# Dividing a conditioning product's 128 rows on VectorE over two feed-forward layers instead of three

## What is computed

```python
def _modulated_norm(h, gain, shift, scale):
    return _rms_norm(h, gain) * (1.0 + scale) + shift

def _swiglu(h, w1, w2):
    a, b = jnp.split(h @ w1, 2, axis=-1)
    return (jax.nn.silu(a) * b) @ w2

ctx = ctx + FFN_RESIDUAL * mc[2, 2] * _swiglu(
    _modulated_norm(ctx, norm_g[i, 2], mc[2, 0], mc[2, 1]), ffn_w1[i, 1], ffn_w2[i, 1])
```

## Time and profile before

| | us |
|---|---|
| median of three executions (2767.69 to 2777.02) | 2773.91 |
| the profiled execution | 2775.72 |
| its span in the trace | 2773.9 |
| up part of `mlp00` | about 66 to 298 |
| up part of `mlp01` | about 913 to 1144 |
| up part of `mlp10` | about 1281 to 1511 |

### The profile page before, as it was taken

How to read it: one execution, slowest core, us unless ns; L and a number is a source line. 1 busy time by engine, 2 the same in 40 slices (tenths; PEclk the granted TensorE clock), 3 DMA queues, 4 the chain that set the end, 5 groups by cost and what they waited for, 6 DMA issues and landing times.

```text
span 2773.9 us, 52909 instructions
## 1 busy us (share of the span) xinstructions
PE 2709.3 (98%) x21984; PEld 2390.5 (86%) x21984; DVE 1454.0 (52%) x2776; ACT 1187.2 (43%) x2123; POOL 1476.2 (53%) x809
## 2 busy tenths in 40 slices
PE   8999999999999999999999999999999999999999
PEld 6888888778888888889888896899998799898999
DVE  4777406656663676505766124453175676613560
ACT  5222225435554322224222245644445666555553
POOL 4444443444334444444444442388886377595887
PEclk9999999999999999999999999999999999999999
DMA  8665432210001455424555326265564253353465
GB/s 308 211 210 196 139 99 84 94 61 4 4 27 61 169 193 169 152 92 146 187 176 173 110 93 137 69 197 185 168 190 151 70 164 118 115 177 128 155 195 160
DMA packets 106549, 384.11 MB, mean 138 GB/s; under 512 B 11431, under 2 KB 16712, under 8 KB 104776
## 3 DMA queue, kind: packets, MB, share of 16 engines
q1 hardware_dynamic: 87880, 313.61, 35.2%
q10 hardware_dynamic: 18432, 67.12, 6.9%
HBM read 375.44 MB, written 5.24 MB: 137 GB/s over the span
## 4 chain that ended last, share of the span: by engine, by line
PE 90%; ACT 3%; DVE 2%; POOL 2%; DMA 1%; issue 1%; SPq 0%; ACTq 0%
PE bank L236 25%; PE bank L238 24%; PE bank L237 24%; PE bank L1088 2%; POOL weights_lo L229 1%; PE upper_banks L236 1%; PE upper_banks L238 1%; PE upper_banks L237 1%; PE upper_banks L1890 1%; PE upper_banks L1873 1%; PE bank L1864 1%; PE upper_banks L1065 1%; PE bank L1202 1%; PE upper_banks L1135 1%; PE upper_banks L1213 1%
## 5 line engine op out<-in xcount | busy, mean ns | idle before, releaser
L229 POOL TENSOR_TENSOR weights_lo<-weights_landing,weights_hi 128x1024 fp32r<-128x1024 f32 x554 | 1341.9, 2427 | 1147.5 <-ACT weights_hi L219 1141.0
L219 ACT ACTIVATE weights_hi<-weights_landing 128x1024 fp32r<-128x1024 f32 x554 | 587.2, 1060 | 1140.7 <-PE bank L238 1032.0
L236 PE MATMUL bank<-normed_hi,weights_lo 128*128 128x256 f32 (+1 forms) x2776 | 922.2, 332 | 6.1 <-ACT normed_hi L707 1.9
L238 PE MATMUL bank<-normed_hi,weights_hi 128*128 128x256 f32 (+1 forms) x2776 | 914.9, 330 | 0.0
L237 PE MATMUL bank<-normed_lo,weights_hi 128*128 128x256 f32 (+1 forms) x2776 | 911.7, 328 | 0.0
L236 PEld LDWEIGHTS bank<-normed_hi,weights_lo 128*128 128x128 f32 x2776 | 522.3, 188 | 66.1 <-issue 4.4
L237 PEld LDWEIGHTS bank<-normed_lo,weights_hi 128*128 128x128 f32 x2776 | 522.4, 188 | 51.6
L238 PEld LDWEIGHTS bank<-normed_hi,weights_hi 128*128 128x128 f32 x2776 | 522.3, 188 | 51.4
L236 PE MATMUL bank<-hidden_hi,weights_lo 128*128 128x256 f32 (+1 forms) x1026 | 339.1, 331 | 0.0
L238 PE MATMUL bank<-hidden_hi,weights_hi 128*128 128x256 f32 (+1 forms) x1026 | 338.6, 330 | 0.0
L237 PE MATMUL bank<-hidden_lo,weights_hi 128*128 128x256 f32 (+1 forms) x1026 | 337.3, 329 | 0.0
(11 more groups left out here) (469 smaller groups left out, 3691.9 us busy)
## 6 DMA issues: line engine op xcount, KB each, us to landing
weights_landing<-w_up SPq DMA_DIRECT2D x176, 512.0 KB, 3.5
ada_rows<-w_ada_rows ACTq DMA_DIRECT2D x128, 512.0 KB, 4.3
weights_landing<-w_down SPq DMA_DIRECT2D x88, 512.0 KB, 3.5
weights_landing<-w_dn SPq DMA_DIRECT2D x33, 512.0 KB, 3.5
weights_landing<-w_mlp_up SPq DMA_DIRECT2D x32, 512.0 KB, 3.5
weights_landing<-w_mlp_down SPq DMA_DIRECT2D x32, 512.0 KB, 3.5
weights_landing<-w_gate SPq DMA_DIRECT2D x24, 512.0 KB, 4.2
weights_landing<-w_xbc SPq DMA_DIRECT2D x24, 512.0 KB, 3.5
```

The lines of the kernel that those rows point to most:

```text
L219: k.nc.scalar.activation(k.WH[:, u % SLOTS, :], k.W[:, u % LANDS, :], ACT.Copy).then_inc(*k.AC.mark(("unit hi", u)))
L229: k.nc.gpsimd.tensor_tensor(k.WL[:, u % SLOTS, :], k.W[:, u % LANDS, :], k.WH[:, u % SLOTS, :].bitcast(F32), ALU.subtract).then_inc(*k.PO. ...
L236: nc.tensor.matmul(out, ll, rh, start=start, stop=False, skip_group_check=True)
L238: return nc.tensor.matmul(out, lh, rh, start=False, stop=stop, skip_group_check=True)
```

## The change

Two thirds of the table change, and one name in a wait of SyncE:

```diff
 ROWS_FIRST = 2 * KT
-ROWS = {"mlp00": (16, 64), "mlp01": (64, 104), "mlp10": (104, 144)}
+ROWS = {"mlp00": (16, 80), "mlp01": (80, 144)}
...
     def rope():
-        sp.wait_ge(*k.DV.after("ada mod", ROWS["mlp10"][1] // KT - 1))
+        sp.wait_ge(*k.DV.after("ada mod", ROWS["mlp01"][1] // KT - 1))
```

## The result

The changed kernel took **2794.92 us** (median; 2792.03 to 2806.58) beside 2773.91 (2767.69 to 2777.71) for the kernel before: ratio **1.0085, 95% interval 1.0057 to 1.0113**, slower by 21.0 us. The forecast was 2785, so slower by 11.0. The sign, the places and the range held; the size was half of what came. The profiled execution of after took 2792.03 us, its span is 2790.2.

What follows compares the result with a forecast made beforehand. TensorE's stream was taken to set the time, with rows free while VectorE keeps pace. Stalls and clock loss, less transposes, 2.8 + 1.7 + 6.0 + 2.2 - 1.7 = +11.0 us, gave 2784.9 on the median of 2773.91; range 2773 to 2802.

Steps and rivals of the forecast that it cites:

- The pair of 11.91 us: `mlp00` and `mlp01`, up part: a three-row pair behind another takes 11.91 us, 0.92 more than TensorE's, its transfer late.
- Lo at 0.69, a wait of 0.8 to 0.9: Sign of being right: lo at 0.69 us once lag exceeds 2, `ada_rows` waits of 0.8 to 0.9 in nearly every three-row pair.
- The lag, forecast 14.9 and 18.1: Raw's start against its undelayed start, at pair 21: 14.9 us late in `mlp00`, 18.1 in `mlp01`.
- rival A: Nothing is late, as lo shortens when GpSimd is idle and lag heals itself: -1.7 us, 2772; chance 0.10.
- the collision that the forecast had: Row transfers starting together with a load of weights, around a lag of 2.9, land later: 1.4 us taken, in `mlp00`.
- The cover of 12.1 us at lo 21: First down tile, step 21: raw 21 may start 12.1 us late before TensorE must wait for lo 21.
- The stalls: TensorE stands still waiting for lo 21: 2.8 us in `mlp00`, 6.0 in `mlp01`, some 0.7 of these at the last up tile.
- Covers that hold: Down part: the seventh unit of weights still arrives before TensorE needs it at step 48, about 4 us to spare.
- The clock, 1.7 and 2.2: TensorE at 1.2 instead of 2.4 GHz behind each stall: 1.7 us lost in `mlp00`, 2.2 in `mlp01`.
- Transposes, -1.7: `mlp10` loses its 16 transposes where TensorE is the bound: -1.7 us.
- B: Rival: the three-row pair takes 11.7 to 11.8 us, so stalls are smaller: +2.6 to +5.4, 2776 to 2780; chance 0.22.
- C: Rival: transfers land later; 0.35 us more each pair gives +24, 2798 (chance 0.14); 1.67 in all 17, +68, 2842 (0.04).

Runs made afterwards that it cites:

- the one with late short operations: The changed kernel with the short scale or gate operation moved behind lo of the next pair, ahead of that pair's rows: 2787.59 us, ratio 1.0053.
- the one with matmuls in the wait: The changed kernel with ten useless matmuls ahead of the wait for lo 21 in the first down tile of `mlp00` and `mlp01`: 2791.4 us, 1.0077.
- The kernel with 61 and 61 rows: The changed kernel with rows divided 61, 61 and 6 over `mlp00`, `mlp01` and `mlp10`: 2774.89 us, ratio 1.0011.

## Why the prediction was right in sign and half in size

**The pair of 11.91 us.** Right, a little small. The pairs of three rows behind three in after take mostly 11.9 to 12.1, 12.0 in the middle. The transfer is what is late, as said: with it a pair earlier the pair takes 10.98. The two pairs of two rows came out at 9.29 and 9.30 (forecast 9.28).

**Lo at 0.69, a wait of 0.8 to 0.9.** The lo is right, the wait was written wrongly: 2.1 to 2.4, since a lo that ends 1.3 us sooner leaves that much more to wait. The start of the first row, 4.24 after raw, is what I should have named; it is 4.2 to 4.4.

**The lag, forecast 14.9 and 18.1, measured 21.7 and 21.9.** Here the sum fails. Up to pair 2 it holds: +0.8 and +5.6 (forecast 0.8 and 5.4). From pair 2 to 21 after takes 229.68 us in `mlp00` against 208.74: +20.9, forecast 12.7 + 1.4. The 6.8 more are: the three short operations that GpSimd holds up, 1.65 + 1.08 + 1.16 = 3.9, a term that I put at nothing though rival A's own row showed the mechanism; transfers that came later than the others, by 0.6, 0.6 and 1.8 (waits of 2.78, 2.80 and 3.97 where 2.2 is usual), 3.0 for the 1.4 I had; and the rest, 1.3, is the 12.0 in place of 11.91 in 17 pairs. A part of this rest is a short operation that nothing holds up: last in its pair it costs 0.2 us (7.89 us from the first row to the next raw, 7.68 without it), and I had left that out too. In `mlp01` it is +16.4 for +12.7: 1.1 of the 3.7 more by the short operation that is held up, 0.6 by three that stand last in a pair and are not (pairs 2, 10 and 13), 0.7 by a later transfer in pair 12 (10.36 where 9.66 is usual), and 1.3 by pairs that are some 0.1 longer each.

The later transfers are in part the collision that the forecast had. Pair 3 of `mlp00` in after, with SyncE's load of weights, ScalarE's transfers 0.6 us behind it, and the first row on VectorE:

```profile
102.43 5.94 SPq L3301 DMA_DIRECT2D weights_landing<-w_up  x2
103.06 1.30 ACTq L611 DMA_DIRECT2D ada_rows<-w_ada_rows  x3
107.20 1.28 DVE L625 CUSTOM_DVE_ANT_0 ada_products<-ada_rows,upper_banks,k_cond_pack 128x1024 f32<-128x1024 f32 x1 [2.78 <-DMA ada_rows<-w_ada_rows]
```

Take the twelve stages with 61 to 66 rows whose transfers are issued three ahead. A pair's first transfer that was issued together with such a load or up to 2.25 us behind it took 4.1 us to landing in the middle (36 of them, 3.6 to 5.9), every other one 3.5 (216 of them). The waits of 2.78 and 2.80 in after are two of the 36 (0.6 and 2.2 us behind a load), and so is pair 12 of `mlp01` (2.0 behind): with 1.2 us in `mlp00` the collision had the size that I gave it, 1.4. But ten of the 216 took over 3.8 us as well, up to 5.5, with no load just before them, and the wait of 3.97 at 182.22 is of this kind; its 1.8 us are what the term lacked, and its cause is open. Such waits come and go: the kernel with 64 rows in `mlp00` alone has 4.12 at 110.78, 3.63 at 185.06 and a third of 3.34 there, the one with late short operations 3.33 at 117.88 and 4.05 at 271.22, the one with matmuls in the wait none over 2.8 in `mlp00` and one of 3.92 in `mlp01`. Up to step 21 three of these kernels run the same instructions in `mlp00`, and their lags are 19.7, 21.7 and 24.5: the term changes by some 5 us from run to run, so the kernel's time does too, and a forecast can give it a size but not a value.

**The cover of 12.1 us at lo 21.** Right: 12.0. It is the same in every kernel.

**The stalls.** Forecast 2.8 and 6.0, so lag less cover; the step was right and had 6.8 and 3.8 too little in it. The trace shows only 4.67 and 4.74 at step 21, where 2.8 and 5.3 were forecast, and taken alone these would mislead: 3.3 us stand ahead of it in `mlp00`, at three raws (2.1 us; forecast only for the last tile of `mlp01`) and at one wait for GpSimd's low part that I had not foreseen at all. ScalarE, which runs in order, stood with `hidden_hi` 20 until raw 20 and came to the third down unit's high part late (ScalarE's own and its DMA issues, after):

```profile
306.98 0.63 ACT L797 ACTIVATE hidden_hi<-silus 128x512 fp32r<-128x512 f32 x1 [9.13 <-DVE silus L808]
306.99 1.30 ACTq L611 DMA_DIRECT2D ada_rows<-w_ada_rows  x3
308.39 1.06 ACT L219 ACTIVATE weights_hi<-weights_landing 128x1024 fp32r<-128x1024 f32 x1 [0.78 <-DVE hidden_lo L810]
```

"Covers that hold" looked at the seventh unit and missed the third. It cost nothing here, by the formula, since it is shorter than the stall that would stand behind it. The kernel with 61 and 61 rows, lag 10.1, has no such wait and lost nothing.

**The clock, 1.7 and 2.2.** 1.9 and 2.6: right in size, by the experiment that keeps TensorE busy. For `mlp00` that is partly luck: 1.7 was meant for a stall of 2.8 us, and the stall was 4.67.

**Transposes, -1.7.** -1.5.

**The rivals.** A (nothing late) is excluded: lo is short as it says, and the wait takes its place. B is excluded by the pairs of 12.0. By the forecast's own list of signs against it three came: waits for `ada_rows` over 1.2 us (1.3 us of each are my slip about lo), TensorE idle in the up part (2.1 us in `mlp00`), and one wait for weights in each down part. C was the right direction for the rest: transfers and port together made the pair 0.36 us longer in `mlp00` (6.8 over 19 pairs) and 0.19 in `mlp01`, nearly its smaller case of 0.35; it would have given 2798, the result is 2795. I had looked for it in the bandwidth alone, and in `mlp00` more than half of it came from what GpSimd holds up. That 2795 lies so near C's 2798 is partly luck: there each lag was to grow by 6 us, by the same 0.35 in every pair, and it grew by 6.8 and 3.8, in `mlp00` mostly by single events.

## What to carry to other kernels

A change that raises the rate of fetched work turns on the prefetch's distance and not on the average of busy time: with the distance of three rows and three rows a pair, each pair waits for a transfer that is issued only in that pair, 2.2 us of its 3.5, and the same kernel with one more ahead loses nothing. Lag adds up over a stage, so small terms that one occurrence hides (a 0.17 us operation held for 1.8) have to be counted through all pairs, and the loss is whatever of the sum exceeds the cover at the tightest point. Measure such a change by its stages, from one instruction to another: where nothing is late they repeat to 0.2 us, and where they don't, as with these transfers, that is itself a finding.

## What the runs showed of the hardware

- A VectorE operation on 128x16 values takes 0.17 us alone and 1.25 to 1.82 beside GpSimd's low part of weights, in four of four cases ending within 0.04 us of GpSimd's instruction (19 of 19 in the kernels with 61 to 66 rows together). The rows' own operation, 1.28 us with one input in SBUF and one in PSUM, keeps its time beside the same GpSimd instruction (297.46 and 298.67, with GpSimd at work from 296.50 to 301.29).
- TensorE's clock: after idle time from 315.7 the matmuls at 320.36 to 324.0 run at 0.63 us and those from 324.64 at 0.40. With ten matmuls in the idle time the granted clock stays at 1.00. The loss was 1.4 to 2.6 us for seven stalls of 4.6 to 5.0 us, and nothing for one of 1.32 us.
- A transfer of 512 KB from ScalarE's queue, first of its pair, landed 3.5 us after its issue in the middle of 216, and 4.1 in the middle of the 36 that were issued together with a load of weights or up to 2.25 us behind it.
- Three transfers issued by ScalarE at 306.99 took 1.30 us of its queue, and its next activation, which stands behind them in the program, started at 308.39, 0.10 us after the last and 0.78 after the activation before had ended. The profile names lo 20 as what released it (it ends at 308.34); the program has no wait for it there, but no run separates the two.
